# Router of a mixture-of-experts layer: the first gathers begin with the rounded rows, the 0/1 matrix is made tile by tile, and the remainders of the turned rows move behind it

## What is computed

```python
def _moe(x, router, w_gate, w_up, w_down):
    logits = (xf @ router).astype(jnp.float32)
    top_v, top_i = lax.top_k(logits, TOP_K)
    gates = jax.nn.softmax(top_v, axis=-1)
    combine = jnp.sum(jax.nn.one_hot(top_i, N_EXPERTS) * gates[..., None], axis=1)
    for e in range(N_EXPERTS):
        y = y + combine[:, e:e + 1] * _swiglu(xf, w_gate[e], w_up[e], w_down[e])
```

## Time and profile before

| | before |
|---|---|
| median of 3 runs | 1587.24 us (1586.83 to 1588.4) |
| the profiled execution: its time, its span | 1586.26 us, 1584.7 us |
| TensorE busy | 98% of the span |
| TensorE's mean granted clock | 0.998 of full speed |
| from the last step of `sel` to the first expert matmul | 597.5 us to 606.8 us of the span |

### The profile page before, as it was taken

The page is one execution under the profiler, slowest core; times in us unless marked ns, Lnnn a source line. Parts: engine busy times, 40 slices in busy tenths (PEclk is TensorE's granted clock), DMA queues, the critical chain, the costliest instruction groups (busy, mean ns, idle before and its releaser), DMA issues.

```text
span 1584.7 us, 23362 instructions
## 1 busy us (share of the span) xinstructions
PE 1559.7 (98%) x8491; PEld 1376.4 (87%) x8491; DVE 1239.0 (78%) x1410; ACT 1024.2 (65%) x1185; POOL 62.4 (4%) x97
## 2 busy tenths in 40 slices
PE   9999999999999999999999999999999999999996
PEld 8999999999989998888787888887888887888885
DVE  5477544444475678999898989988988988998996
ACT  4455333333354557788687878777778777778875
POOL 1002100000020010000200000000000001000100
PEclk9999999999999999999999999999999999999999
DMA  9624954444534345999999999999999999999992
GB/s 269 203 80 140 372 185 144 147 151 140 160 107 134 107 140 188 375 372 379 399 396 382 385 370 379 395 396 344 385 369 377 395 390 377 382 394 384 387 392 73
DMA packets 229902, 457.44 MB, mean 289 GB/s; under 512 B 10930, under 2 KB 73088, under 8 KB 229760
## 3 DMA queue, kind: packets, MB, share of 16 engines
q1 hardware_dynamic: 224288, 434.16, 75.8%
q0 software_dynamic: 5520, 22.04, 3.6%
HBM read 441.74 MB, written 17.58 MB: 290 GB/s over the span
## 4 chain that ended last, share of the span: by engine, by line
PE 92%; DVE 4%; DMA 1%; ACT 1%; issue 1%; SPq 0%; DVEq 0%; ACTq 0%
PE ps L1037 18%; PE ps L1012 12%; PE ps L1014 12%; PE ps L1013 12%; PE ps L663 11%; PE ps L665 11%; PE ps L664 11%; DVE wlo L1459 2%; PE ps L1050 2%; DMA raw<-in_moe_w_down 1%; DMA proj<-in_x_prompt 0%; PE ps L1086 0%; DVE x L1557 0%; DVE x L1525 0%; PE ps L818 0%
## 5 line engine op out<-in xcount | busy, mean ns | idle before, releaser
L1459 DVE TENSOR_TENSOR wlo<-raw,whi 128x1024 fp32r<-128x1024 f32 x672 | 778.8, 1219 | 47.8 <-ACT whi L1140 46.7
L1140 ACT ACTIVATE whi<-raw 128x1024 fp32r<-128x1024 f32 x672 | 676.2, 1055 | 68.2 <-PE ps L1037 45.7
L1012 PE MATMUL ps<-whi,xg 128*128 128x512 f32 x896 | 354.1, 395 | 1.0 <-DVE wlo L1459 1.0
L1014 PE MATMUL ps<-whi,xg 128*128 128x512 f32 x896 | 349.6, 390 | 0.0
L1013 PE MATMUL ps<-wlo,xg 128*128 128x512 f32 x896 | 349.0, 390 | 0.0
L1454 DVE TENSOR_TENSOR wlo<-raw,whi 128x2048 fp32r<-128x2048 f32 x72 | 165.1, 2295 | 126.3 <-ACT whi L1136 126.2
L663 PE MATMUL ps<-xh,whi 128*128 128x320 f32 x832 | 259.6, 312 | 1.0 <-DVE xl L1543 1.0
L665 PE MATMUL ps<-xh,wlo 128*128 128x320 f32 x832 | 257.1, 309 | 0.0
L664 PE MATMUL ps<-xl,whi 128*128 128x320 f32 x832 | 257.1, 309 | 0.0
L1014 PEld LDWEIGHTS ps<-whi,xg 128*128 128x128 f32 x896 | 168.1, 188 | 35.8
L1012 PEld LDWEIGHTS ps<-whi,xg 128*128 128x128 f32 x896 | 168.3, 188 | 34.9 <-issue 1.4
(11 more groups left out here) (346 smaller groups left out, 1420.7 us busy)
## 6 DMA issues: line engine op xcount, KB each, us to landing
raw<-in_moe_w_gate SPq DMA_DIRECT2D x112, 1024.0 KB, 8.2
raw<-in_moe_w_up SPq DMA_DIRECT2D x112, 1024.0 KB, 8.5
raw<-in_moe_w_down SPq DMA_DIRECT2D x112, 1024.0 KB, 7.9
raw<-in_w_in SPq DMA_DIRECT2D x23, 1024.0 KB, 6.3
raw<-in_ffn_w_gate SPq DMA_DIRECT2D x14, 1024.0 KB, 5.0
raw<-in_ffn_w_up SPq DMA_DIRECT2D x14, 1024.0 KB, 5.0
raw<-in_ffn_w_down SPq DMA_DIRECT2D x14, 1024.0 KB, 5.1
raw<-in_w_out SPq DMA_DIRECT2D x8, 1024.0 KB, 5.2
```

Of the source, the lines that this page charges most:

```text
L1012: pe.matmul(bank[:], xh_k, wh, start=k == 0, stop=False)
L1014: mm = pe.matmul(bank[:], xl_k, wh, start=False, stop=k == KT - 1)
L1140: act.activation(part(whi, n, SPLIT, h), part(raw, n, RAW, h), ACT.Copy).then_inc(hi_ready, 1)
L1459: dve.tensor_tensor(part(wlo, n, SPLIT, h), part(raw, n, RAW, h), part(whi, n, SPLIT, h).bitcast(F32), ALU.subtract).then_inc(lo_ready, 1)
```

## The change

The first two gathers, g = 0 and 1, begin with `xt_hi` alone (`part` 0), each matmul behind the tile of `pick` that it needs; the totals are summed behind these 12 matmuls; then come the 12 with `xt_lo` (`part` 1), each behind its half tile. Gathers 2 and 3 stay in one piece each, their `xt_lo` matmuls waiting half tile by half tile. The five `keep_busy` matmuls ahead of the first gather are gone. VectorE makes one remainder ahead of `pick` in place of three, two behind `pick`, one behind the totals, and the last two behind its reads of gathers 0 and 1. One half tile moves from bank 7 to bank 1, the small sums from bank 1 to bank 0.

```diff
-        XT_BANK = {0: 6, 2: 7, 4: 3, 1: 4, 3: 5, 5: 2}
+        XT_BANK = {0: 6, 2: 1, 4: 3, 1: 4, 3: 5, 5: 2}
...
-                pe.matmul(ps[1][:, 0:E * TT], before[:], sel_by(0, TT), start=True, stop=False)
+                pe.matmul(ps[0][:, 0:E * TT], before[:], sel_by(0, TT), start=True, stop=False)
                 for t in range(1, TT):
-                    pe.matmul(ps[1][:, E * t:E * TT], ones[:], sel_by(0, TT - t), start=False, stop=t == TT - 1)
+                    mm = pe.matmul(ps[0][:, E * t:E * TT], ones[:], sel_by(0, TT - t), start=False, stop=t == TT - 1)
+                mm.then_inc(pos_done, 1)
+
+                pe.wait_ge(cleared, 5)
+                pe.wait_ge(acc_ready, 1)
+                for g in range(2):
+                    gather(g, 0, lambda t: pe.wait_ge(pick_ready, t + 1))
+                pe.wait_ge(rt_step, RT_SEL + 1)
                 for t in range(TT):
-                    mm = pe.matmul(ps[1][:, E * TT:E * TT + E], ones[:], sel_by(t, t + 1), start=t == 0, stop=t == TT - 1)
+                    mm = pe.matmul(ps[0][:, E * TT:E * TT + E], ones[:], sel_by(t, t + 1), start=t == 0, stop=t == TT - 1)
                 mm.then_inc(pos_done, 1)
-
-                keep_busy(BUSY["first gather"], ps[0])
-                pe.wait_ge(cleared, 5)
-                pe.wait_ge(pick_ready, 1)
-                for g in range(GATHERS):
-                    pe.wait_ge(xtl_ready, TT if g < 2 else 2 * TT)
-                    if g < 2:
-                        pe.wait_ge(acc_ready, g + 1)
-                    if g >= 2:
-                        pe.wait_ge(job_read, g - 1)
-                    gather(g, ps[6 + g % 2])
+                for g in range(2):
+                    gather(g, 1, lambda t: pe.wait_ge(xtl_ready, t + 1))
+                for g in range(2, GATHERS):
+                    pe.wait_ge(job_read, g - 1)
+                    pe.wait_ge(xth_ready, 2 * TT)
+                    gather(g, 0)
+                    gather(g, 1, lambda t: pe.wait_ge(xtl_ready, TT + t + 1))
...
-                xt_rest(0, TT)
+                xt_rest(0, 1)
                 dve.wait_ge(pos_done, 1)
...
                 make_pick(qpos)
-                xt_rest(TT, 2 * TT)
-                step(dve.tensor_copy(over_n[:, 0:E], ps[1][:, TT * E:TT * E + E]))
-                for g in range(GATHERS):
+                xt_rest(1, TT)
+                dve.wait_ge(pos_done, 2)
+                step(dve.tensor_copy(over_n[:, 0:E], ps[0][:, TT * E:TT * E + E]))
+                xt_rest(TT, TT + 1)
+                read_gather(0)
+                read_gather(1)
+                xt_rest(TT + 1, 2 * TT)
+                for g in range(2, GATHERS):
                     read_gather(g)
...
-                full = [P, TT, 2, P]
-                dve.tensor_tensor(pick[:], slot_no[:].unsqueeze(1).unsqueeze(1).to_broadcast(full),
-                                  tab[:, :, at].unsqueeze(3).to_broadcast(full), ALU.is_equal).then_inc(pick_ready, 1)
+                full = [P, 2, P]
+                for t in range(TT):
+                    dve.tensor_tensor(pick[:, t, :, :], slot_no[:].unsqueeze(1).to_broadcast(full),
+                                      tab[:, t, at].unsqueeze(2).to_broadcast(full), ALU.is_equal).then_inc(pick_ready, 1)
```

More of the change, by code:

```diff
@@ L954, in router @@
                 for t in range(TT):
-                    mm = pe.transpose(ps[1][0:TOK[t], E * t:E * t + E], lgT[:, P * t:P * t + TOK[t]], ident[0:E, 0:E])
+                    mm = pe.transpose(ps[0][0:TOK[t], E * t:E * t + E], lgT[:, P * t:P * t + TOK[t]], ident[0:E, 0:E])
                 mm.then_inc(lg_turned, 1)
@@ L958, in router @@
                     turn_rows(j)
-                keep_busy(BUSY["logits"], ps[0])
+                keep_busy(BUSY["logits"], ps[7])
                 pe.wait_ge(rt_step, RT_SEL)
                 sel_by = lambda a, b: sel[:, a:b, :].rearrange("p t e -> p (t e)")
-                pe.matmul(ps[1][:, 0:E * TT], before[:], sel_by(0, TT), start=True, stop=False)
+                pe.matmul(ps[0][:, 0:E * TT], before[:], sel_by(0, TT), start=True, stop=False)
                 for t in range(1, TT):
-                    pe.matmul(ps[1][:, E * t:E * TT], ones[:], sel_by(0, TT - t), start=False, stop=t == TT - 1)
+                    mm = pe.matmul(ps[0][:, E * t:E * TT], ones[:], sel_by(0, TT - t), start=False, stop=t == TT - 1)
@@ L981, in gather @@
-            def gather(g, bank):
+                for g in range(2):
[5 more added lines that the diff above has]
+                    gather(g, 1, lambda t: pe.wait_ge(xtl_ready, TT + t + 1))
+            def gather(g, part, wait_tile=lambda t: None):
+                bank, xt = ps[6 + g % 2], (xt_hi, xt_lo)[part]
@@ L983, in gather @@
                 for kk in range(2):
                     k = 2 * g + kk
[L985 to L990, removed]
+                    for t in range(TT):
+                        wait_tile(t)
+                        mm = pe.matmul(bank[:, 2 * P * kk:2 * P * kk + 2 * P], xt[:, t, P * k:P * k + P],
+                                       pick[:, t, :, :].rearrange("p a s -> p (a s)"),
+                                       start=part + kk + t == 0, stop=part == 1 and kk == 1 and t == TT - 1)
@@ L992, in pair @@
+                if part:
+                    mm.then_inc(job_done, 1)
             def pair(i, steps, first=False):
@@ L1838, in router @@
                 dve.wait_ge(lg_turned, 1)
-                step(dve.tensor_copy(lg[:, 0:2, :], ps[1][:, 0:2 * E].rearrange("p (t e) -> p t e", e=E)))
-                step(dve.tensor_copy(lg[0:TOK[2], 2, :], ps[1][0:TOK[2], 2 * E:3 * E]))
+                step(dve.tensor_copy(lg[:, 0:2, :], ps[0][:, 0:2 * E].rearrange("p (t e) -> p t e", e=E)))
+                step(dve.tensor_copy(lg[0:TOK[2], 2, :], ps[0][0:TOK[2], 2 * E:3 * E]))
                 full = [P, TT, E, E]
@@ L1856, in router @@
                 assert n == RT_SEL
-                xt_rest(0, TT)
+                xt_rest(0, 1)
                 dve.wait_ge(pos_done, 1)
-                step(dve.scalar_tensor_tensor(out=qpos[:], in0=ps[1][:, 0:TT * E].rearrange("p (t e) -> p t e", e=E),
+                step(dve.scalar_tensor_tensor(out=qpos[:], in0=ps[0][:, 0:TT * E].rearrange("p (t e) -> p t e", e=E),
                                               scalar=1.0, in1=sel[:], op0=ALU.add, op1=ALU.mult))
                 make_pick(qpos)
-                xt_rest(TT, 2 * TT)
-                step(dve.tensor_copy(over_n[:, 0:E], ps[1][:, TT * E:TT * E + E]))
-                for g in range(GATHERS):
+                xt_rest(1, TT)
[6 more added lines that the diff above has]
+                for g in range(2, GATHERS):
                     read_gather(g)
```

## The result

| | before | after |
|---|---|---|
| median of 22 runs each | 1587.95 us (1586.36 to 1589.7) | 1590.18 us (1587.47 to 1593.78) |
| profiled execution: time, span | 1586.26, 1584.7 us | 1592.19, 1590.7 us |
| mean granted clock there | 0.998 | 0.995 |

The ratio is 1.0013, 95% interval 1.0007 to 1.0019: slower by about 2.1 us, within the 0.2% that the forecast called no change, and 1590.18 lies inside its range near the upper end. The spread is what the sum could not give: 6.3 us after, 3.3 us before. The profiled execution of the changed kernel (1592.19 us) is the fourth slowest of its 22, so it lost more time than a middle one. It shows where time can be lost, not how much a typical execution loses.

What follows compares the result with a forecast made beforehand. TensorE, busy 98% of 1584.7 us, was taken as the bound; gather 2 starting 0.63 late and late remainders made +1.53 at the experts, so 1587.24 + 1.5 = 1588.7 us, range 1586.5 to 1590.4.

Steps and rivals of the forecast that it cites:

- no change: Whole kernel's time: a difference within 0.2% or 3.2 us can't be told from none; chance 0.92.
- the sum: Whole kernel: step times added up along the chain to the experts, +1.5 us on 1587.24, giving 1588.7 us.
- First gather: TensorE's first gather matmul, behind ScalarE's copy to `acc`: starts at 599.88, 0.74 us earlier than before.
- Gather 2: Start of the second pair of gathers on TensorE: 604.49 against 603.86 before, 0.63 us later.
- First expert matmul: TensorE's start on the experts behind gather 3: 608.34 against 606.81 before, +1.53 us.
- The stop within gather 2: TensorE, second pair of gathers: `xt_lo` matmuls wait for the last two remainders, a stop of about 1 us.
- VectorE's idle time ahead of `over_n`: VectorE, first pair of gathers: idle from 601.03 to 602.28, waiting for the totals.
- I found no slack: From the gathers to the kernel's end: a shift counts one for one, with nothing between to take it up.
- The two parts, 0.57 and 0.84: Delay before the experts: late gather 2, +0.63 us, and last two remainders behind VectorE's reads, within +1.53 in all.
- Waits on each matmul cost nothing: 36 gather matmuls, a wait on each: taken as 0, upper bound 2.5 us; costly-waits rival, 1591.3 us, chance 0.04.
- the removed useless matmuls were hidden under the wait for `pick` and give nothing: TensorE ahead of the first gather: taking out the five useless matmuls was claimed to gain nothing.
- the 0.03 for the falling clock: Rival: TensorE's idle time at the gathers lowers its clock; 5 us of it gives 1591.2 us; chance 0.03.

Runs made afterwards that it cites:

- x1: Changed kernel with the five useless matmuls put back ahead of the first gather; median 1590.19 us, ratio 1.0015.
- x11: x1 plus three useless matmuls ahead of each of the two waits at each pair's end; median 1587.85 us, ratio 0.9998.
- x9: Kernel before plus three useless matmuls ahead of each of the two waits at each pair's end; median 1586.43 us, ratio 0.9992.
- x3: x1 with all remaining remainders made right behind `pick`, ahead of the totals and VectorE's reads; median 1587.7 us, ratio 1.0007.
- x2: Kernel before without its five useless matmuls ahead of the first gather, nothing else changed; median 1589.54 us, ratio 1.0013.
- x7: x3 without the useless matmuls ahead of the first gather; median 1589.52 us, ratio 1.0009.
- x10: Changed kernel plus three useless matmuls ahead of each of the two waits at each pair's end; median 1589.84 us, ratio 1.0015.
- x5: Changed kernel with gathers 0 and 1 one after the other, totals and three useless matmuls ahead of them, VectorE's steps reordered; median 1586.97 us, ratio 0.9995.
- x6: x1 with three more useless matmuls behind gather 1 and three more within gather 2; median 1589.32 us.
- x8: x5 plus three useless matmuls ahead of each of the two waits at each pair's end; median 1586.23 us, ratio 0.9990.

## Why the prediction came out right, and where it failed

**The sum held.** First gather: 599.57 - 597.30 = 2.27 us behind L963 in x1, 2.30 forecast. Gather 2: 6.73, forecast 6.91. First expert matmul: +1.41, forecast +1.53. The stop within gather 2 is there, and so is VectorE's idle time ahead of `over_n`, 1.16 us in x1 and 1.25 forecast. The shift passes to the end: x11 - x9 is +1.42 in the time itself, so "I found no slack" held. The two parts, 0.57 and 0.84, are measured by x3 (forecast 0.63 and 0.9).

**Waits on each matmul cost nothing,** as taken: 12 with a wait each take 1.66 us in x1, against 1.68.

**The step that failed** is "the removed useless matmuls were hidden under the wait for `pick` and give nothing", and with it the 0.03 for the falling clock. In the profiled executions without filler ahead of the gathers (after, x2, x7, x10) the clock fell at the gathers in three of four; in the eight with it (before, x1, x3, x5, x6, x8, x9, x11) in none. If it were chance which three of the twelve lose it there, all three would be among those four in 4 of 220 cases. The price was 1.2 us (x2), 1.5 (x7 against x3) and 2.7 (after against x1) for 3.4, 3.4 and 6.8 us at 1.2 GHz: under half of the time spent slow, for part of it TensorE would have waited anyway. The evidence that I leaned on, a window with 1.24 us of idle time and the clock at 1.00, was one execution; x10 kept its clock behind a gap of 1.44 us and the changed kernel lost it behind the same one. The Trainium skill's warning ("TensorE: Matmul & The Clock Gate", HAM oscillation) of gaps between trains of matmuls is borne out by these traces. The Trainium skill's own case there has longer gaps than these; here the clock fell at gaps of 1.44 to 1.53 us in three executions of four. I had given it 0.03.

Of the measured +2.1 us the order gives +1.4. The rest isn't shown one by one: x1, with filler ahead of the gathers, is no faster than the changed kernel (ratios 1.0015 and 1.0013). It loses its clock elsewhere, and mostly at the pairs' ends, for with the fillers there (x11) none of its executions has a mean clock as low as 7 of x1's have. That the order and the missing filler don't add to 3.4, as they do in x10 - x9, fits a kernel before whose own executions also lose the clock now and then: the pair fillers take 1.3 us off its median by their ratio, and x10 stands no better against before than the changed kernel does. I have no run that says why fillers at the pairs' ends help less where the one ahead of the gathers is missing. That the median fell inside the range at all was in part luck. The range has no term for the clock, and 10 of the 22 executions are above its upper end of 1590.4. The spread that I counted with, 1.6 us from three runs, was 3.3 with 22, and the median of the kernel before moved from 1587.24 to 1587.95.

**Open:** why weights come late near 765 to 800 us, and more so (3.9 to 4.2 us of TensorE's waits, not 1.6 to 2.5) in the profiled executions of the changed kernel, x2 and x10. x7, without filler too, isn't among them, and x10 is, though its clock didn't fall at the gathers: neither the missing filler nor the fallen clock decides it alone. x10 and x11 differ in the five useless matmuls only. From 614 to 755 us they issue every weight load 0.19 to 0.21 us apart, with durations that agree to 0.01 us; the next pair of issues parts them, x10 first:

```profile
759.15 6.88 SPq L428 DMA_DIRECT2D raw<-in_moe_w_up  x2
...
759.34 3.24 SPq L428 DMA_DIRECT2D raw<-in_moe_w_up  x2
```

So nothing that the issues show is handed on from the gathers to the late weights.

## What to carry to other kernels

Before you take out work that fills an engine's idle time, ask what else depends on that engine being busy; TensorE's clock was at half here behind waits of 1.44 to 1.53 us, and behind two of 0.98 and 0.82 us close together. Useless matmuls in the latter moved no start at the gathers (x9, shift 0.00) and took 1.3 us by the ratio (0.9983 to 1.0001) off a kernel that wasn't suspected. When a pipeline's first item is started earlier, look at when it is complete: two gathers interleaved by halves both finish late, and the bank of the first is freed late; one after the other (x5) gave -0.35 where interleaving gave +0.57 with the remainders early (x3) and +1.41 with two of them late (x1). With a small effect, first make the spread small, then measure: x9 and x11 show the order's part by itself, 1.0 to 1.4 us, which the first comparison could not.

## What was not expected of the hardware

Executions of one kernel differ by up to 6 us, and the slower ones have the lower mean clock: the mean granted clock of the changed kernel's 22 runs went from 0.998 (1587.51 us) to 0.992 (1593.78 us). A kernel's profile at a clock of 1.00 is one execution and does not vouch for the next. A fall at half clock was also seen behind a 1.96 us wait for weights (x5, 779 us), with matmuls every 0.43 us. The best version here, x8, has a median of 1586.23 us, 0.9990 of the kernel before (0.9981 to 1.0000), and a range of 1.6 us; only x9's is narrower, 1.4.
